# First attention of a fused two-block transformer: VectorE masks both heads of a pair before its other work, and the compressed scores' passes stand in four pieces

## The reference, cut to what matters

```
h = x @ w_in_even[li]
qa, ka, va, qn, kc, vc, ksl, vsl, kw, vw, g = _split(h, EVEN_SPLITS)
o_a = diff_attention(...)   # 4 heads x 2 parts: softmax(q k) of part 0 less lam times that of part 1, times v
o_b = nsa_attention(...)    # 8 heads; gates weigh three branches: compressed, selected, window
mix = jnp.concatenate([o_a, o_b], axis=-1) @ w_out_even[li]
x = layer_norm(ALPHA * x + mix, ...)
```

```
kc = partial_rope(compress(k_cmp, 0), cmp_end)      # n_cmp = (256 - 32) // 16 + 1 = 15
vc = compress(v_cmp, 1)
scores = q . kc ; masked softmax ; times vc ; times the gate
```

## Time and profile before

| what | value |
|---|---|
| time, median of three | 1354.55 us (1351.98 to 1357.73) |
| the profiled execution: time, span | 1355.96 us, 1354.3 us |
| mean granted TensorE clock | 0.993 of full speed |
| TensorE busy | 98% of the span |
| VectorE busy, ScalarE busy | 47%, 18% |
| `a0` in the trace | first scores at 73.35 us, last values at 150.42 us |

### The profile page before, as it was taken

One profiled execution on the slowest core, in us unless ns is written; L12 is line 12 of the kernel. 1 busy time (PEld: TensorE's weight loads), 2 busy tenths in 40 slices (PEclk: granted clock), 3 DMA queues, 4 the chain that ended last, 5 costly groups with the idle time before them and its releaser, 6 DMA issues.

```text
span 1354.3 us, 18984 instructions
## 1 busy us (share of the span) xinstructions
PE 1330.4 (98%) x7306; PEld 823.3 (61%) x7306; DVE 641.7 (47%) x1224; ACT 243.1 (18%) x573; POOL 89.1 (7%) x114
## 2 busy tenths in 40 slices
PE   9999999999999999999999999999999999999996
PEld 8677575786747856586686675744444444444433
DVE  1226589877862257977979263421221222212213
ACT  2135311211102450120123162100000000000002
POOL 1116500000000120000000100000000000000001
PEclk9997999999999999999999999999999999999999
DMA  9931154565453414676574405399999999999994
GB/s 381 354 109 65 64 205 178 219 237 216 183 197 150 157 45 190 236 292 263 221 276 168 158 34 216 147 421 419 421 421 413 422 421 421 422 420 421 421 421 195
DMA packets 51006, 359.53 MB, mean 265 GB/s; under 512 B 5888, under 2 KB 6096, under 8 KB 8432
## 3 DMA queue, kind: packets, MB, share of 16 engines
q1 hardware_dynamic: 45248, 324.60, 59.5%
q0 software_dynamic: 5392, 32.05, 6.6%
q10 hardware_dynamic: 288, 1.80, 0.3%
HBM read 356.88 MB, written 1.05 MB: 264 GB/s over the span
## 4 chain that ended last, share of the span: by engine, by line
PE 82%; DVE 7%; issue 1%; ACT 1%; DVEq 0%; ACTq 0%
PE ps L1470 13%; PE ps L980 13%; PE ps L971 11%; PE ps L1499 7%; PE ps L1395 7%; PE ps L1448 7%; PE ps L953 5%; PE ps L794 4%; PE ps L799 2%; PE ps L873 2%; PE ps L892 1%; PE ps L831 1%; PE ps L1355 1%; PE ps L1224 1%; PE ps L1241 1%
## 5 line engine op out<-in xcount | busy, mean ns | idle before, releaser
L2698 DVE TENSOR_TENSOR masked_and_probs<-ps,gate_rows 128x512 f32<-128x512 f32 x52 | 33.5, 686 | 152.4 <-PE ps L1499 152.4
L794 PE MATMUL ps<-xT,ring 128*128 128x256 f32 x432 | 94.7, 380 | 0.8 <-DVE xT L1992 0.8
L1448 PE MATMUL ps<-masked_and_probs,probT 128*128 128x512 f32 x208 | 94.4, 594 | 1.0 <-DVE masked_and_probs L2698 1.0
L1395 PE MATMUL ps<-masked_and_probs,mix_rows 128*128 128x256 f32 (+1 forms) x416 | 93.0, 376 | 0.0
L1395 PEld LDWEIGHTS ps<-masked_and_probs,mix_rows 128*128 128x128 f32 x416 | 75.0, 190 | 28.8 <-issue 19.6
L971 PEld LDWEIGHTS ps<-xT,ring 128*128 128x128 f32 x768 | 87.8, 192 | 3.8 <-issue 3.8
L1607 ACT ACTIVATE qk_tiles<-ps 64x256 f32<-64x256 f32 (+3 forms) x84 | 39.2, 468 | 278.0 <-PE ps L971 241.8
L794 PEld LDWEIGHTS ps<-xT,ring 128*128 128x128 f32 x432 | 81.5, 190 | 12.3 <-ACT xT L1595 1.0
L971 PE MATMUL ps<-xT,ring 128*128 128x128 f32 x768 | 88.7, 275 | 0.0
L980 PE MATMUL ps<-ring,qk_tiles 128*128 128x512 f32 x192 | 85.2, 592 | 0.0
L953 PE MATMUL ps<-ring,xT 128*128 128x512 f32 x192 | 83.8, 593 | 0.0
(11 more groups left out here) (469 smaller groups left out, 2260.8 us busy)
## 6 DMA issues: line engine op xcount, KB each, us to landing
ring<-in_stream SPq DMA_DIRECT2D x200, 1024.0 KB, 8.6
qk_tiles<-in_stream SPq DMA_DIRECT2D x46, 1024.0 KB, 20.3
v_rows<-in_ada POOLq DMA_DIRECT2D x12, 1024.0 KB, 5.1
qk_tiles<-in_ada POOLq DMA_DIRECT2D x12, 1024.0 KB, 5.2
vec_rows<-in_stream SPq DMA_DIRECT2D x12, 1024.0 KB, 17.2
con<-in_stream SPq DMA_DIRECT2D x12, 1024.0 KB, 18.2
y_rows<-in_stream SPq DMA_DIRECT2D x12, 1024.0 KB, 19.7
par<-in_stream SPq DMA_DIRECT2D x12, 1024.0 KB, 20.8
```

The source lines that it names most:

```text
L794: mm = pe.matmul(ps[0:n, bank, off:off + T], w[:, kk, col:col + n], src[:, k, :], start=bank not in started, stop=k == KT - 1, skip_group_ ...
L1395: mm = pe.matmul(ps[:, 5 + kk // 2, kk % 2 * 2 * P:kk % 2 * 2 * P + width], h2[:, t, k * P:(k + 1) * P], select[:, t, 0:width], start=t == ...
L1448: mm = pe.matmul(ps[:, q, :], probT[:, buf, 256 + q // 2 * P:256 + (q // 2 + 1) * P], yslot[:, q % 2 * 512:(q % 2 + 1) * 512], start=False ...
L2698: dve.tensor_tensor(yslot[:, cols], ps[:, 5 + half, :], gaterow[:, 1, cols], ALU.mult).then_inc(ready, 1)
```

## The change

VectorE: `attention("a0")` does the masks of units i and i+1 one after the other in the even step, ahead of the copy, the group work and the hook of that step; the odd step has only its copy, group work and hook. The other two attentions keep their order. `compressed_masked` moves from step 21 to step 22, and `compressed_max` joins `compressed_less_max` on step 23.

TensorE: `compressed_scores` becomes four pieces of two products (one query tile and one key head's two head pairs each), on steps 17, 19, 20 and 21. The two pieces of the first head pairs no longer wait for `s_ropeb`, the rotated second half of the queries.

```diff
-            def compressed_scores():
+            def compressed_scores(half, qt):
                 pe.wait_ge(s_projsb, 6)
-                pe.wait_ge(s_ropeb, 1)
+                if half:
+                    pe.wait_ge(s_ropeb, 1)
+                else:
+                    pe.wait_ge(s_roped, 4)
                 pe.wait_ge(s_ckey, 2)
-                for qt in range(TT):
-                    for pair in range(4):
...
+                for pair in range(2 * half, 2 * half + 2):
+                    at = (4 * qt + pair) * 2 * NCMP
+                    mm = pe.matmul(ps[:, 6, at:at + 2 * NCMP], qk[:, 8 + pair, qt * P:(qt + 1) * P],
+                                   kblock[:, pair // 2, :, :].rearrange("p o n -> p (o n)"), start=True, stop=True)
+                if half and qt:
+                    mm.then_inc(s_cpe, 1)
...
-                12: [lambda: queries(1, 1, 1)], CMP_AT: [compressed_scores], CMP_AT + 8: [turn_compressed],
+                12: [lambda: queries(1, 1, 1)], CMP_AT - 3: [lambda: compressed_scores(0, 0)],
+                CMP_AT - 1: [lambda: compressed_scores(0, 1)], CMP_AT: [lambda: compressed_scores(1, 0)],
+                CMP_AT + 1: [lambda: compressed_scores(1, 1)], CMP_AT + 8: [turn_compressed],
...
             def compressed_less_max():
+                compressed_max()
                 dve.tensor_tensor(by_key, by_key, cmax.unsqueeze(2).to_broadcast(per_key), ALU.subtract).then_inc(s_csub, 1)
...
                 for i in range(a, b + (6 if name == "a0" else 7)):
-                    if i < b:
-                        kind, qt, h, nk, _, _, _ = UNITS[i]
...
+                    for j in range(i, i + 2) if name == "a0" and i % 2 == 0 else range(i, i + (name != "a0")):
+                        if j < b:
+                            masked_scores(j)
                     u = i - 3
...
-                             ROPE_AT[1]: lambda: rotated_queries(1), CMP_AT + 1: compressed_masked, CMP_AT + 2: compressed_max,
-                             CMP_AT + 3: compressed_less_max, CMP_AT + 5: compressed_factors,
+                             ROPE_AT[1]: lambda: rotated_queries(1), CMP_AT + 2: compressed_masked, CMP_AT + 3: compressed_less_max, CMP_AT + 5: compressed_factors,
```

More of the change, by code:

```diff
@@ L2138, in compressed_weighed, with masked_scores @@
                 dve.tensor_tensor(by_key, by_key, csums.unsqueeze(2).to_broadcast(per_key), ALU.mult).then_inc(s_cprob, 1)
+            def masked_scores(i):
+                kind, qt, h, nk, _, _, _ = UNITS[i]
+                _, _, mask, _ = unit_operands(i)
+                dve.wait_ge(s_sc, i + 1)
+                if i >= 4:
+                    dve.wait_ge(s_exp, i - 3)
+                first = negsink[:, h:h + 1] if kind == "loc" else 1e38
+                dve.tensor_tensor_reduce(out=masked[:, i % 4, 0:nk], in0=scores(i)[:, 0:nk], in1=mask,
+                                         scale=-1.0 if kind == "fox" else -SCALE, scalar=first,
+                                         op0=ALU.add, op1=ALU.min, accum_out=negmax[:, i:i + 1]).then_inc(s_mask, 1)
             def attention(name, hooks):
```

## The result

The changed kernel takes 1360.05 us, the median of 22 executions (1352.87 to 1362.55), against 1356.12 us for the kernel before (22 executions, 1351.52 to 1358.57). The ratio is 1.0029 with a 95% interval of 1.0018 to 1.0041: slower by 3.9 us, where +1.6 us was forecast, and inside the 0.5% that the prediction took for no change. It lies outside the range of the case that the forecast named (1353.5 to 1358.5) and inside the wider one (1351.0 to 1361.0), by 1 us.

What follows compares the result with a forecast made beforehand. TensorE, busy in 98% of the span, bounds the kernel; VectorE costs only where TensorE waits for it. +1.7 us in the last eight pairs and -0.15 up to pair 28 gave +1.6: 1356.0 us, range 1351.0 to 1361.0.

Steps and rivals of the forecast that it cites:

- the case that the forecast named: Late copies in `a0` and one fall of the clock: +1.6 us, 1353.5 to 1358.5 us, chance 0.5.
- the signs that the prediction itself named for being wrong: Low stretch in `a0` missing, several microseconds longer or coming twice; or pairs from 36 on keeping 1.50 and 1.79 us.
- The late copies: Pairs 32 to 46 of `a0`: the second mask ahead of the copy delays it and lengthens the pairs, +1.7 us.
- the rival of the hidden copies: In most of the last pairs the copy waits for its transpose anyway; only small gains left, 1354.0 us, chance 0.15.
- Pairs 14 to 28: Waits for the second mask vanish, against late copies at 24 and 26: -0.3 us, half left at low clock, -0.15.
- the piece of step 17: At pair 18: it falls into the 0.46 us freed from the mask wait and gives that gain back.
- The late mask of pair 24: Maximum and subtraction on step 23 lie ahead of it: covered at 1.2 GHz, late by 0.45 us at 2.4 GHz.
- The waits in total: In `a0`, the values' waits for the copy grow from 2.0 to some 3.5 us.
- Second fall: 0.15: Rival: pairs 36 to 46, longer with the same passes, fill TensorE more thinly and the clock falls again; chance 0.15.
- The other rival: The clock does not fall in `a0`, or much later, as 30-column passes are thinned out: 1352.0 us, chance 0.2.
- The rule that was weighed: Half rate only for an idle or cold TensorE: filling changes nothing in a busy stretch, no second fall, +1.6 us.

Runs made afterwards that it cites:

- the two kernels with one part each: Against the kernel before: VectorE's order with the compressed scores in one piece, ratio 1.0039; the four pieces with the masks in the old order, ratio 0.9998.
- the second trace of the changed kernel: The changed kernel run once more, nothing altered, for a trace of another execution: 1360.09 us, ratio 1.0032; the traced execution took 1362.2 us.
- the first group of experiments: Follow-up kernels that share their runs of the kernel before, whose median there was 1352.5 us over 35 executions.
- the last six pairs alone: The kernel before, its one piece and hooks kept, with both masks first in pairs 36 to 46 only: 1359.9 us, ratio 1.0042.

## Why the prediction was right, and where its size was off

The measured time lies in the range, and that is in part luck. The case that was forecast, late copies and one fall of the clock, is not what most executions did, and the upper end of the range reaches 1361.0 only because it took in half of a rival. Of the signs that the prediction itself named for being wrong two came: no low stretch in the first trace, and two in the second. Its account of the instructions' order held; its account of the clock did not.

**The late copies.** Forecast +1.7 us for pairs 32 to 46. Measured in the changed kernel's first trace: pairs 36 and 38 at 1.66 us (forecast 1.65), 40 and 42 at 2.13 (2.12), 44 at 2.49 (forecast 0.3 more; before it took 144.92 - 142.74 = 2.18). From the scores of pair 36 to the turn inside the output projection it is 26.65 us (131.31 to 157.96), against 25.11 (136.16 to 161.27) in the kernel before, whose clock was full there, and 25.11 (131.65 to 156.76) in the four pieces with the old order: +1.54 us. Pairs 32 and 34 add 0.09 (4.02 against 3.93), forecast 0.1. This step stood, and the rival of the hidden copies is out.

**Pairs 14 to 28.** Forecast -0.4 us by pair 22, measured -0.45; that the piece of step 17 takes up the freed wait is what the two kernels with one part each show. From pair 14 to pair 32 it is 27.26 us before (104.97 to 132.23) and 27.00 in the second trace of the changed kernel (104.73 to 131.73), each with 13.6 us at 1.2 GHz: -0.26, forecast -0.15. The late mask of pair 24 at 2.4 GHz, forecast as a cost only for a clock that does not fall, is there: 2.54 us against 1.79, with the copy's delay of 0.3 in it.

**The waits in total.** Forecast 3.5 us for the values, from 2.0. These rows are of PEld, the weight loads, which overlap the products (in pair 40 above the load waits 0.71 us and the product 0.52); that TensorE lost 2.0 us there was a misreading. In the kernel before its products waited much less for the copies:

```profile
PE ps L907 <- DVE probT L2164: 0.2, 1, 0.2
```

The changed kernel, first trace, weight loads and then products:

```profile
PEld ps L907 <- DVE probT L2175: 7.7, 16, 1.1
PE ps L907 <- DVE probT L2175: 4.3, 12, 0.9
```

And its second trace:

```profile
PEld ps L907 <- DVE probT L2175: 4.8, 12, 0.7
PE ps L907 <- DVE probT L2175: 1.9, 6, 0.5
```

The first ran all of `a0` at 2.4 GHz, where pairs 24 to 30 wait as well; the number was worked out for a trace with the first low stretch. Even there it was too small.

**The step that was mis-sized** is the weight of a rival. "Second fall: 0.15", and one fall as the likeliest case, gave +1.6 us. Of the 32 timed executions of the changed kernel 8 have a clock of at least 0.996 and a median of 1353.8 us; in the first 22, the 17 others have a median of 1360.7. Against the heaps of the kernel before, measured beside them, that is 2.0 us more in the lower heap, close to the +1.6, and 4.4 us more in the upper one (1360.7 against 1356.3; 1356.2 in the first group of experiments). The 2.4 us between the two I put down to the second fall, which cost 3.8 us where it was traced. That not every execution of the upper heap had one would explain the rest, but it is not shown: only two executions of the changed kernel were traced. The mechanism and the reason (the same passes in longer pairs) were in that rival, and the place too: the fall was seen at 143.5 and, with the last six pairs alone, at 138. Its chance was under-estimated. I had read the clock of pairs 36 to 46 as 1.00 in one execution and taken that for an argument against it. What the runs show is that little was missing: an added 0.16 to 0.34 us a pair was enough in most executions.

The price by the forecast's own 32% of the slow time would be 3.3 us for the 10.2 us of the second stretch; it was 3.8. At its end TensorE has products that follow one another without a wait, and they cost about twice as much: the eight transposes of the first half of the mixed rows took 1.92 us instead of 1.04. Two thirds of this rival's chance were given to a time beyond 1361.3 us; 7 of the 24 executions of the upper heap lie there, and the median does not.

**The other rival** was right too, in a quarter of the executions (8 of 32): the clock does not fall, forecast 1352.0 us, measured 1353.8. Its reason, the 30-column passes thinned out, is not borne out: the pieces alone had a clock of at least 0.996 in 7 of 12 executions, the kernel before in 24 of 35. And it took for a gain of the change what the kernel before does as well in many executions: both traces of the kernel before had a fall, and 55 of its 87 executions in the three groups had no long one.

**The rule that was weighed.** The idle products have no use but to fill, and in three of the four kernels that had them in pairs 22 to 26 every execution kept a clock of at least 0.996. The second trace of the changed kernel fell twice with no wait for a copy longer than 0.5 us (the row above), while the first had one of 0.9 and did not fall. So the length of the single wait does not decide.

The Trainium skill ("TensorE: Matmul & The Clock Gate", section "What's actually happening") lists half rate for an idle or cold engine and full rate for a busy one. Read as idle against busy alone, as the prediction read it, the second fall should not be there; the trace disagrees, and the measurement decides. The same section says that the rate is set "based on how busy the PE has been recently", which leaves room for the filling of a stretch to count, and with that the runs agree.

## What to carry to other kernels

In a loop over two engines, find the one instruction that the other engine waits for, and put nothing between it and what releases it; work that nobody waits for, here the second mask, belongs behind it, except where a longer piece of side work would otherwise come ahead of both. Where TensorE's stretch is sparse, a few tenths of a microsecond more in each round can cost a fall of the clock that is dearer than the waits, so look at several executions' granted clock before calling a stage safe. When the times of a kernel form two heaps, compare heap with heap; the median alone mixes their places with their shares. A useless product in a gap that exists anyway can be the cheapest cure, and it is also a good test of whether the clock is the cause.

## What the runs showed of the hardware that was not expected

- The granted clock fell to 1.2 GHz while TensorE worked: the largest single wait near the second fall was 0.52 us. The first low stretch in `a0` began between 115.0 and 121.0 us in the traces that had one, and lasted from 3.5 to 14 us; some executions of the same kernel had none.
- Whether it falls differs from execution to execution and from kernel to kernel. A mean clock of at least 0.996 had 55 of 87 executions of the kernel before, 8 of 32 of the changed one, 0 of 6 with the last six pairs alone, and 12 of 12 in three of the four kernels with five small idle products in pairs 22 to 26 (11 of 12 in the fourth).
- With the four pieces, five idle products of 128 and 256 columns (10 records more, at most 2.1 us if nothing hid them) made the median 0.14% shorter.
